# Order of the block's last work and the weight splits, at two stage ends of a two-block transformer kernel

## What is computed

```python
# first block: l = 0, 1
h = rms_norm(x, ffn2_norm[l])
x = x + 0.5 * swiglu(h, ffn2_w_gate[l], ffn2_w_up[l], ffn2_w_down[l])
# second block: l = 0, 1
h = rmsnorm(x, g_mix_pre[l]) * (1.0 + scale_a) + shift_a
y = hybrid_mixer(h, w_in[l], ...)          # three causal attentions
x = x + gate_a * rmsnorm(y, g_mix_post[l])
h = rmsnorm(x, g_ffn_pre[l]) * (1.0 + scale_f) + shift_f
x = x + gate_f * rmsnorm(swiglu_2(h, w_gate_up[l], w_down[l]), g_ffn_post[l])

def swiglu(h, w_gate, w_up, w_down):
    return (jax.nn.silu(h @ w_gate) * (h @ w_up)) @ w_down
```

## Time and profile before

| | us |
|---|---|
| median of 3 runs | 1626.58 (1626.2 to 1627.04) |
| the profiled execution's own time | 1628.62 |
| its span, first to last instruction | 1626.7 |
| PE busy in it | 1589.7 (98%) |
| DVE busy | 1095.1 (67%) |
| ACT busy | 874.6 (54%) |
| GpSimd busy | 99.9 (6%) |
| DMA: bytes moved, mean rate | 332.14 MB, 204 GB/s |
| mean granted clock of TensorE, of full speed | 0.997 |

### The profile page before, as it was taken

How to read it: one execution, slowest core, us unless ns; L and a number is a source line. 1 busy time by engine, 2 the same in 40 slices (tenths; PEclk the granted TensorE clock), 3 DMA queues, 4 the chain that set the end, 5 groups by cost and what they waited for, 6 DMA issues and landing times.

```text
span 1626.7 us, 21863 instructions
## 1 busy us (share of the span) xinstructions
PE 1589.7 (98%) x8052; PEld 1316.4 (81%) x8052; DVE 1095.1 (67%) x1788; ACT 874.6 (54%) x1655; POOL 99.9 (6%) x163
## 2 busy tenths in 40 slices
PE   8999999999999999999899999999999989999998
PEld 7888887688888888887678888888788879878886
DVE  7767677676767766678676766677645566775454
ACT  7444567654435444467664444767444466774342
POOL 0000022100000000020210000011000000210000
PEclk9999999999999999999999999999999999999999
DMA  9888743277877778764158877643665545256551
GB/s 368 291 288 275 203 146 130 91 261 266 275 271 199 266 262 275 255 164 137 58 199 274 285 267 205 194 131 118 208 196 178 188 159 176 78 181 225 189 179 54
DMA packets 96569, 332.14 MB, mean 204 GB/s; under 512 B 14545, under 2 KB 15057, under 8 KB 95953
## 3 DMA queue, kind: packets, MB, share of 16 engines
q1 hardware_dynamic: 77472, 277.91, 51.4%
q10 hardware_dynamic: 18992, 52.83, 10.2%
HBM read 329.64 MB, written 1.06 MB: 203 GB/s over the span
## 4 chain that ended last, share of the span: by engine, by line
PE 91%; DVE 3%; POOL 2%; DMA 2%; ACT 1%; issue 1%; DVEq 0%; POOLq 0%; ACTq 0%
PE PS L875 27%; PE PS L876 26%; PE PS L877 26%; PE PS L953 2%; PE PS L1080 1%; PE PS L1122 1%; DMA raw<-in_ffn 1%; POOL st L2253 1%; PE PS L1058 1%; PE PS L1218 1%; PE PS L1219 1%; PE PS L1220 1%; PE PS L893 1%; DVE Wl L1748 1%; PE PS L1054 1%
## 5 line engine op out<-in xcount | busy, mean ns | idle before, releaser
L1748 DVE TENSOR_TENSOR Wl<-raw,Wh 128x1024 fp32r<-128x1024 f32 (+1 forms) x302 | 353.5, 1212 | 33.0 <-ACT Wh L1355 32.4
L875 PE MATMUL PS<-Wh,Hh 128*128 128x512 f32 (+1 forms) x824 | 322.8, 392 | 4.9 <-DVE Hl L1808 3.9
L877 PE MATMUL PS<-Wh,Hl 128*128 128x512 f32 (+1 forms) x824 | 319.1, 387 | 0.0
L876 PE MATMUL PS<-Wl,Hh 128*128 128x512 f32 (+1 forms) x824 | 318.8, 387 | 0.0
L1355 ACT ACTIVATE Wh<-raw 128x1024 fp32r<-128x1024 f32 (+1 forms) x302 | 301.4, 1049 | 17.5 <-PE PS L877 10.7
L1748 DVE TENSOR_TENSOR QTl<-raw,QTh 128x1024 fp32r<-128x1024 f32 x192 | 224.7, 1205 | 23.4 <-ACT QTh L1355 22.9
L1441 ACT ACTIVATE WK<-PS,st 128x256 f32<-128x256 f32 x88 | 41.6, 474 | 330.8 <-PE PS L877 330.8
L875 PE MATMUL PS<-QTh,Hh 128*128 128x512 f32 (+2 forms) x536 | 209.6, 391 | 2.4 <-DVE Hl L1808 1.7
L877 PE MATMUL PS<-QTh,Hl 128*128 128x512 f32 (+2 forms) x536 | 207.0, 386 | 0.0
L876 PE MATMUL PS<-QTl,Hh 128*128 128x512 f32 (+2 forms) x536 | 206.8, 386 | 0.0
L1355 ACT ACTIVATE QTh<-raw 128x1024 fp32r<-128x1024 f32 x192 | 191.9, 1044 | 5.2 <-DMA raw<-in_ffn 2.5
(11 more groups left out here) (250 smaller groups left out, 2304.0 us busy)
## 6 DMA issues: line engine op xcount, KB each, us to landing
raw<-in_ffn SPq DMA_DIRECT2D x396, 512.0 KB, 5.6
BT<-in_ada ACTq DMA_DIRECT2D x96, 512.0 KB, 4.4
raw<-in_win SPq DMA_DIRECT2D x64, 512.0 KB, 4.8
raw<-in_wo SPq DMA_DIRECT2D x32, 512.0 KB, 5.3
raw<-in_win SPq DMA_DIRECT2D x8, 420.0 KB, 4.0
raw<-in_lat SPq DMA_DIRECT2D x6, 512.0 KB, 6.3
BT<-in_nab SPq DMA_DIRECT2D x2, 1024.0 KB, 7.9
raw<-in_win SPq DMA_DIRECT2D x8, 256.0 KB, 2.8
```

The costliest lines, as they stand in the source:

```text
L875: e.matmul(out_, xh, wh, start=start, stop=False)
L876: e.matmul(out_, xh, wl, start=False, stop=False)
L877: return e.matmul(out_, xl, wh, start=False, stop=stop)
L1748: ins = e.tensor_tensor(low(p)[:, 0:w], raw[p % RAW][:, 0:w], high(p)[:, 0:w].bitcast(f32), ALU.subtract)
```

## The change

In a stage that a stage from 6 on follows, the event that scales X of tile 0 moves from behind the last "gu" to behind the last "turn". Three rules are added to `weights_to`: the last "gu" of such a stage and the scaling event of tile 0 bring no splits, and the second chunk of the last but one group's "down" of tile 1 may bring four.

```diff
                ("down", y - 1, 1, (0, 1)), ("gu", y, 1, 0), ("turn", z, 0, 0), ("down", y, 0, (0, 1)), ("down", z, 0, (0, 1)),
-               ("turn", y, 1, 0), *end[0], ("gu", z, 1, 0), *scale[0]]
+               ("turn", y, 1, 0), *end[0], ("gu", z, 1, 0)]
         if nlate:
-            ev += [("down", y, 1, (0,)), ("turn", z, 1, 0), ("down", y, 1, (1,)), ("down", z, 1, (0, 1)), *nxt]
+            ev += [("down", y, 1, (0,)), ("turn", z, 1, 0), *scale[0], ("down", y, 1, (1,)), ("down", z, 1, (0, 1)), *nxt]
...
                         goal = (0, 6, 8, 8, 9)[i] if s == 0 and i < 5 else n + room(ev)
+                        if ev[0] == "gu" and ev[1] == NG - 1 and ev[2] and s + 1 in range(6, len(STAGES)):
+                            goal = n
+                        if ev[0] == "xs" and ev[1] % 2 == 0:
+                            goal = n
+                        if ev == ("down", NG - 2, 1, (1,)) and s + 1 in range(6, len(STAGES)):
+                            goal = n + 4
```

## The result

| | us |
|---|---|
| changed kernel, median of 8 runs | 1631.63 (1630.20 to 1634.38) |
| kernel before, median of 8 runs beside it | 1626.9 (1626.1 to 1628.28) |
| ratio | 1.0027 (95% interval 1.0019 to 1.0036) |
| the profiled execution's own time | 1632.74 |
| its span | 1630.8 |

The change makes the kernel slower by 0.27%, 4.4 us (3.1 to 5.9) by the ratio; the two medians lie 4.7 us apart. I had forecast 2.7 us and a range up to 1631.0: the direction was right, the size too small, and the time lies 0.6 us above the range. Half of these 0.6 us is the kernel before, which ran at 1626.9 beside it and not at the 1626.58 from which I had counted.

A forecast was written before the change was run, and what follows sets the result against it. PE, holding 91% of the chain of waits, was taken to bound the kernel by its work and standstills. Terms: 2.07 - 0.74 + 1.4 = +2.7 us, so 1626.58 becomes 1629.3 us, range 1627.1 to 1631.0.

The forecast's parts named there:

- What bounds the kernel, and where the change acts: Whole kernel: PE's work plus its waits set the time, and the change acts at the ends of stages 5 and 7.
- End of stage 7: PE's holds of 1.28 and 1.50 us go, but DVE's splits then delay the first NW: gain 0.74 us.
- End of stage 5: Two QTl leave DVE's hole for its full stretch, so NW and PE's projection come later: loss 2.07 us.
- What is put off costs nothing: Stages 6 and 8: splits done later, and the loads behind them, hold nothing up: price 0.
- TensorE's clock: Stages 6 and 8: emptier pauses make the clock fall, costing about 0.9 and 0.5, together 1.4 us, bounds 0 and 3.4.
- the list of signs: Profile signs at both ends, among them the first NW about 7.4 us behind stage 5's last turn, before 5.5.
- No fall of the clock: Rival, both ends: the clock stays up, the order costs 2.07 and gives 0.74, so 1627.9 us; chance 0.22.
- Slower by over 0.2%: Rival, stages 6 and 8: clock falls as PE takes up each projection, 3.4 us worked at 1.2 GHz; +4.3, 1630.9; chance 0.24.

The follow-up runs named there:

- with the clock held up: Eleven zero matmuls put in PE's pause at each changed end; ratios to the kernel before: both ends 1.0006, stage 5's end only 1.0012, stage 7's only 0.9997.
- stage 5 alone: Against the changed kernel, only the end of stage 5 is changed and stage 7 ends as before; ratio 1.0024 to the kernel before.
- one split fewer: Against the changed kernel, DVE does one Wl less ahead of the first NW at both ends; ratio 1.0009 to the kernel before.
- the kernel with the pauses filled: The changed kernel plus eleven zero matmuls on PE behind the transposes of tile 0 at both ends; ratio 1.0006 to the kernel before.

## Why the prediction was wrong

- *What bounds the kernel, and where the change acts.* Right. The two ends hold the loss; the stretches between them differ by under 1 us each in the two profiled executions, and by 0.7 in all.
- *End of stage 7.* Right. Both holds went, PE was through with the stage 4.32 us behind the turn (4.35 in the working), and the gain that was left is 0.76 us (0.74 forecast), since DVE's run of five splits was late next. One split fewer in that run makes the pause 1.15 us shorter, so the run is what PE waits for.
- *End of stage 5.* Right: +2.06 in the profile (2.07 forecast), +2.0 in time with the clock held up. (NW came 7.54 us behind the turn. The working gives 7.55; the list of signs, which has "about 7.4", took it too low.)
- *What is put off costs nothing.* Right. With the clock held up the distance from first projection to first exponential is 39.5 to 39.7 us at both stages, with the late splits in place (39.50 and 39.67 before).
- *TensorE's clock.* This step failed in its size: the term of 1.4 us was too small, while the mechanism (an emptier pause, then a fall to 1.2 GHz) was right. The working said that "a fall of 3.4 us costs at most half of it, 1.7 us", took 0.9 and 0.5, and bounded both together at 3.4. Measured in the profile: 2.40 and 1.14, 3.54 together, above even that bound. Two errors are in it. First, I took too much off the price of one fall. A single fall of 3.4 us cost 1.43 and 1.21 us at stage 6 (stage 5 alone; one split fewer) and 1.04 to 1.16 at stage 8, so with single falls the term would have been 2.2 to 2.6. I held the first matmuls to be paced by DVE's Hl anyway, but that is 0.69 us for three, and at 1.2 GHz three take 1.05. I counted on part of the fall to lie in the pause, which it did in none of the single falls. And the 0.38 us at stage 8 is the idle time of the weight loads; PE's last matmul ahead of these transposes starts at 1332.02, the next could follow at 1332.25, and they start at 1332.36, so PE itself had only 0.11 us to give. Second, at stage 6 the low clock lasted 6.8 us, twice as long as each of the falls near 281, 783 and 793 in the kernel before; a longer fall I had not allowed for.
- *The rivals.* "No fall of the clock" is the kernel with the pauses filled, +1.0 us (-0.3 to +2.4) against its +1.33, so its price was right and its premise wrong. "Slower by over 0.2%" has a sum, +4.3, that nearly meets the +4.4, and I gave it 0.24. That is in part luck: it had two falls of 3.4 us, each begun just as PE takes up the projection, and 3.0 us for both, while the profile has one of 6.8 us begun 0.8 us before and one of 3.4 begun 0.6 us after. I had the right mechanism and set it at under half of its size, then drew the range around that.
- *The Trainium skill's rule* ("TensorE: Matmul & The Clock Gate", section "HAM oscillation — how this bites in real kernels") is that PE's clock is put back when it idles between bursts, and that the next burst starts cold. It was the better guide than the one stretch of this trace that had stayed at full clock: the runs show a fall behind every empty pause of 2.29 us and more at these ends, none behind those of 1.37 us and less, and 1.00 behind the filled ones. That the burst starts cold they show only at stage 6 of the changed kernel; in the five other falls at these ends PE's first matmuls still ran at full clock for 0.1 to 1.5 us.

What stays open: why the low clock lasted twice as long in the profiled execution of the changed kernel at stage 6 and not in that of stage 5 alone. One difference is on record: the long fall is the only one at these ends that began while PE still stood in its pause. With one such execution that is a hint and no proof. The mean clocks speak for long falls in other runs too: by the estimate above it is three lengths of 3.4 us per run of the changed kernel, and 1.6 per run, not one, of the kernel with stage 5 alone, whose runs lie between a clock of 0.996 (1630.0 to 1631.5 us) and 0.994 (1632.5 to 1633.1 us). Only the profiled executions show the place.

## What to carry to other kernels

When work is moved out of a wait, ask in which other wait of the same engine it used to hide, and count it again there: at stage 5 two splits left a free hole and cost 2.0 us, and at stage 7 some 3.25 us of freed PE time shrank to 0.76 because splits that had run in PE's waits now stood ahead of the next stage's first operand. Move ahead of such an operand only what it needs, and spread the rest over the engine's own pauses. And do not price the pauses of TensorE by their sum: three holds of 1.28, 1.50 and 0.92 us, 3.7 us in all, with matmuls between them kept the full clock, while one of 3.4 us, and even one of 2.3, cost another 1.0 to 2.4 us. Eight transposes stood ahead of every pause before a projection, of the harmless ones (0.92 to 1.37 us) too; whether that matters no run here tells.

## What the runs showed of the hardware that I had not expected

- A fall of the granted clock lasted 6.8 us, though PE was at work in the last 6 of them: 0.50 and 0.59 in two stretches of 3.4 us one after the other. The other falls at these ends lasted 3.4 us.
- A fall is not tied to the end of the pause. In the profiles of these ends it began between 0.8 us before and 1.5 us behind the first matmul after the pause.
- A fall of 3.4 us cost 1.0 to 1.4 us, less than the 1.7 of half its length.
- Eleven matmuls of zeros, 2.79 us of work that nobody reads, made the program 3.4 us faster than the same program without them (1.0006 against 1.0027).
- A pause of 2.29 us behind eight transposes was followed by 0.52, at both ends of the same execution. One of 1.37 us, or of 1.15, was not.
